# Products of ones on TensorE in four of its idle times, in a transformer block and mixture of experts on one core

## The reference

```python
def rmsnorm(x, g):
    y = xf * lax.rsqrt(jnp.mean(xf * xf, axis=-1, keepdims=True) + EPS)
    return (y * g.astype(jnp.float32)).astype(x.dtype)

def first_block(...):
    x = x + even_mixer(rmsnorm(x, e_norm[j]), ...)          # the first norm
    x = x + memory_cross_attention(rmsnorm(x, c_norm[i]), ...)
    ...
def second_block(...):
    x = x + merged @ w_out[l]
    h2 = rms_norm(x, ffn_norm_g[l])
    x = x + hierarchical_moe(h2, ...)                       # router, 32 experts, top 2
    return rms_norm(x, final_norm_g)                        # the last norm
```

## Time and profile before

| | |
|---|---|
| median of 3 runs | 1638.87 us (1638.64, 1643.22, 1638.87) |
| the profiled execution's own time | 1638.95 us |
| its span, first to last instruction | 1637.1 us |
| mean granted TensorE clock | 0.989 |
| PE busy | 1595.3 us (97%) |
| DVE, ACT, POOL busy | 845.6, 583.0, 547.6 us |

### The profile page before, as it was taken

How to read it: one execution, slowest core, us unless ns; L and a number is a source line. 1 busy time by engine, 2 the same in 40 slices (tenths; PEclk the granted TensorE clock), 3 DMA queues, 4 the chain that set the end, 5 groups by cost and what they waited for, 6 DMA issues and landing times.

```text
span 1637.1 us, 20086 instructions
## 1 busy us (share of the span) xinstructions
PE 1595.3 (97%) x7426; PEld 1203.3 (73%) x7426; DVE 845.6 (52%) x1456; ACT 583.0 (36%) x963; POOL 547.6 (33%) x239
## 2 busy tenths in 40 slices
PE   7999999999999999999999999999999999999997
PEld 5888768887888888887877667888877885444543
DVE  5447577125655546344668686343242644343434
ACT  4127454334332225324533342343243333112213
POOL 4441226731444444751334123455424410000000
PEclk9999999999999999999999999999999999999998
DMA  5331223521332323441222113334312349999991
GB/s 187 95 99 39 77 77 119 165 90 59 97 96 90 103 91 98 150 127 50 76 81 72 39 45 97 110 115 130 94 61 90 127 191 365 410 422 423 421 418 68
DMA packets 52787, 235.94 MB, mean 144 GB/s; under 512 B 6240, under 2 KB 7136, under 8 KB 48096
## 3 DMA queue, kind: packets, MB, share of 16 engines
q1 hardware_dynamic: 48960, 222.60, 38.8%
q0 software_dynamic: 2016, 7.34, 1.1%
q10 hardware_dynamic: 1728, 4.87, 0.9%
HBM read 230.59 MB, written 4.19 MB: 143 GB/s over the span
## 4 chain that ended last, share of the span: by engine, by line
PE 90%; DVE 6%; issue 2%; ACT 2%; DMA 0%; SPq 0%; DVEq 0%; ACTq 0%
PE G L1803 69%; PE O L1803 7%; PE S L1803 6%; PE TR L1803 4%; PE TR L1913 2%; DVE sumsq L993 1%; PE G L2370 1%; DVE sq L1053 1%; DMA w_ring<-in_stream_dram 0%; ACT hi_ring L569 0%; DVE U L1024 0%; DVE sumsq L1123 0%; DVE arena L1423 0%; DVE U L1780 0%; DVE arena L1202 0%
## 5 line engine op out<-in xcount | busy, mean ns | idle before, releaser
L534 POOL TENSOR_TENSOR lo_ring<-w_ring,hi_ring 128x1024 fp32r<-128x1024 f32 x219 | 533.9, 2439 | 788.9 <-ACT hi_ring L569 788.6
L569 ACT ACTIVATE hi_ring<-w_ring 128x1024 fp32r<-128x1024 f32 x219 | 231.3, 1059 | 588.7 <-PE G L1803 584.5
L1803 PE MATMUL G<-xa_hi,hi_ring 128*128 128x512 f32 x928 | 378.4, 408 | 9.7 <-DVE xa_lo L1115 9.6
L1803 PE MATMUL G<-xa_lo,hi_ring 128*128 128x512 f32 x928 | 364.6, 393 | 0.0
L1803 PE MATMUL G<-xa_hi,lo_ring 128*128 128x512 f32 x928 | 364.1, 392 | 0.0
L1803 PEld LDWEIGHTS G<-xa_hi,hi_ring 128*128 128x128 f32 x928 | 175.1, 189 | 50.1 <-issue 12.2
L1803 PEld LDWEIGHTS G<-xa_lo,hi_ring 128*128 128x128 f32 x928 | 175.1, 189 | 39.1 <-issue 2.6
L1803 PEld LDWEIGHTS G<-xa_hi,lo_ring 128*128 128x128 f32 x928 | 174.8, 188 | 39.4
L1803 PE MATMUL G<-yb_hi,hi_ring 128*128 128x512 f32 x388 | 154.4, 398 | 3.1 <-ACT arena L667 2.2
L1803 PE MATMUL G<-yb_hi,lo_ring 128*128 128x512 f32 x388 | 151.7, 391 | 0.0
L1803 PE MATMUL G<-yb_lo,hi_ring 128*128 128x512 f32 x388 | 151.3, 390 | 0.0
(11 more groups left out here) (350 smaller groups left out, 2503.8 us busy)
## 6 DMA issues: line engine op xcount, KB each, us to landing
w_ring<-in_stream_dram SPq DMA_DIRECT2D x219, 512.0 KB, 3.5
arena<-in_w_gu_dram SPq DMA_DIRECT2D x16, 2048.0 KB, 11.7
ex_rings<-in_w_dn_dram SPq DMA_DIRECT2D x40, 512.0 KB, 15.6
ex_low<-in_w_gu_dram SPq DMA_DIRECT2D x8, 2048.0 KB, 18.1
ex_rings<-in_w_gu_dram SPq DMA_DIRECT2D x8, 2048.0 KB, 15.7
arena<-in_w_dn_dram SPq DMA_DIRECT2D x16, 512.0 KB, 14.0
sq<-in_w_dn_dram SPq DMA_DIRECT2D x8, 512.0 KB, 17.6
X<-in_x_in_dram SPq DMA_DIRECT2D x8, 256.0 KB, 5.8
```

The source lines that it names most:

```text
L534: nc.gpsimd.tensor_tensor(lo_ring[:, s, :], w_ring[:, s, :], hi_ring[:, s, :], ALU.subtract).then_inc(low, 1)
L569: nc.scalar.activation(hi_ring[:, m % RING, :], w_ring[:, m % RING, :], ACT.Copy).then_inc(high, 1)
L1803: return nc.tensor.matmul(*args, **kw)
```

## The change

A helper issues products of a matrix of ones with itself, in plain float32, into a PSUM bank that nothing reads before it is written anew. It is called in four places (and with `final` once more in a branch that this input does not take): eight products of 512 columns ahead of everything else on PE, three of 256 ahead of the wait for the assignment, three of 256 between the rank products and the gather, and three of 256 between the last column sums and the last broadcast. Nothing waits for them, and they wait for nothing of their own.

```diff
+            def idle_products(bank, n, width):
+
+                for _ in range(n):
+                    mm(bank[:, 0:width * P].rearrange("p (a b) -> p a b", a=width), ones[:, :],
+                       ones[:, 0:P].unsqueeze(1).broadcast_to([P, width, P]), start=True, stop=True)
+
+            idle_products(S[:, 1, :], 8, 4)
+
             def three(out_ap, n, cols, hi, lo, first, last, weights_move=False):
...
             router(KT - 1)
             for f in range(4, KT):
                 rows(f)
+            idle_products(S[:, 1, :], 3, 2)
             pe.wait_ge(m_ready, 1)
             pe.wait_ge(rk_tab, 2)
...
                 ins.then_inc(col_full, 1)
+                idle_products(S[:, 1, :], 3, 2)
                 pe.wait_ge(diag, BC["f2"] + 1 + again)
                 mm(TR[:, :], ones[:, :], RB[:, :], start=True, stop=True).then_inc(bc_full, 1)
 
+            idle_products(O, 3, 2)
             gather_first()
             slots_first()
```

## The result

| | before | after |
|---|---|---|
| median | 1640.31 us (1637.46 to 1644.75, 22 runs) | 1644.24 us (1639.20 to 1646.91, 22 runs) |
| ratio | | 1.0017, 95% interval 1.0009 to 1.0025 |
| span of the profiled execution | 1637.1 us | 1642.5 us |

A forecast was written before the change was run, and what follows sets the result against it. PE, busy 97% of the span, was taken as the bound. Terms 0 - 0.75 + 0 and 0 = -0.75 on 1638.95 gave 1638.2, set to 1638.1 us as the median was 0.08 lower; range 1635.6 to 1641.0.

The forecast's parts named there:

- term 3: Fill between ranks and gather: clock holds, gather gains 1.8 us, slot table limits it; -0.75 us reaches the first expert products.
- Term 1: Eight products at the start: tile 1 ends about 1 us earlier, column sums still wait for the sum of squares; 0.
- Rival B: Clock falls at the first column sums as PE's wait there grows; +1.3 us, total 1639.4; chance 0.22.
- Terms 2 and 3: Fill ahead of the ranks hides in the assignment wait, 0; fill ahead of the gather keeps the clock up, -0.75 us.
- Term 4: Three products ahead of the last broadcast: fill at half clock ends 1.1 us late; taken as 0, between +1.1 and -1.0.
- C: Fills themselves run at half clock: gather ends +1.0 us, last fill +1.1, total 1641.0; chance 0.10.
- D: Falls at 216, 274 and 666 us, 1.7 us each, move: one or two vanish, 1636.4 or 1634.7, or one added; chance 0.15.
- E: No effect: clock falls at 1349.1 all the same, or experts' loads absorb the shift; 1638.9; chance 0.08.
- The Trainium skill's rule on transposes: Full clock "doesn't engage for transpose-mode": both rank fills would run at half clock, 1.0 us slower; given a small chance.

The follow-up runs named there:

- e15: Before plus twenty products of ones of 128 columns at the start, nothing elsewhere; executed once, 1643.59 us.
- e18: Before plus twenty products of ones of 128 columns behind the expert loop, ahead of the last broadcast; executed once, 1646.20 us.
- e8: Before plus fills at the start, ahead of the first column sums, three later norms' sums and one projection, and the two around the ranks; 1640.44 us, 0.9988.
- e14: The change plus two products of 256 columns between the gather and the slot products; 1642.49 us, 1.0001 of before.
- e17: The change unaltered, measured again against before; 1643.58 us, 1.0012.
- e1: Before plus only the change's eight products at the start; 1641.72 us, 1.0001.
- e3: Before plus only the change's three products ahead of the last broadcast; 1641.77 us, 1.0000.
- e11: Before plus the change's two fills around the ranks and two products of 256 columns ahead of the slot products; 1641.12 us, 0.9998.
- e10: e8 plus two products of 256 columns ahead of the slot products, without the last fill; 1639.39 us, 0.9985 of before.
- e9: The change plus two products of 512 columns ahead of the first column sums and two of 256 ahead of the slot products; 1640.06 us, 0.9989 of before.
- e16: Before plus twelve wide products in seven places, none at the start or ahead of the last broadcast; 1641.47 us, 1.0001.
- e4: Before plus the eight products at the start and two of 512 columns ahead of the first column sums; 1640.71 us, 0.9991.
- e5: Before plus only the change's start fill and last fill; 1642.33 us, 1.0005.
- e6: Before plus only fills ahead of three later norms' column sums and one projection; 1641.05 us, 0.9992.

## Why the prediction was wrong

The step that failed is the end of term 3: "**-0.75** reaches the first expert products" and "There PE is the bound to the end". The gain did reach the first expert products (-1.09 in the profile), and the loop behind them gave it back: rows that come 0.8 to 1.1 us late and, in some executions, a fall at its start. With it failed the level that all was added to, 1638.87, and of the loss itself 0.8 to 1.6 us stay open. By the ratio the change cost 2.8 us where the sum had -0.75.

**All profiles together** give what the two alone could not. Mean times, with the number of profiles (left out: e15's start, 32.80, with its own fill, and e18's end, where its fill stands):

| stretch | kernels | us |
|---|---|---|
| to the first broadcast's end | change's start fill, sums' wait not covered (5) | 34.62 |
| | neither (6, before among them; before 32.19) | 34.56 |
| | sums' wait covered (8) | 32.58 |
| `ffn` sums to first expert product | no fills at the ranks (9) | 23.04 |
| | fills there (11) | 22.23 |
| expert loop | rows on time (10) | 257.1 |
| | rows late, no fall (7) | 257.8 to 258.4 |
| | rows late and a fall at its start (3: e8, e14, e17) | 259.7 to 260.5 |
| last sums to the end | last fill (7) | 16.45 |
| | none (12) | 16.25 |

**Term 1, the start: 0.** Right, and so was its working: the sums start when they did and the second unit's low part is waited for. The mean to the first broadcast is the same with and without it (34.62 and 34.56), and e1 gives 1.0001.

**Rival B.** In the profiled execution it happened, where it was said. Its price was too low: the fall lasted 6.8 us and not 3.4, and cost 3.25 us instead of 1.3. In all profiles together a fall of 3.4 us here costs 1.6 and one of 6.8 costs 3.2: from the start of the sums to the end of the broadcast 7.5, 9.1 and 10.7 us. Its condition, "It decides as soon as tile 1 ends 1 us earlier", was not what sets the kernels apart. Of the twelve profiles without a cover here, the ten in which PE waited 1.62 to 2.35 us all had a fall within 2.4 us of the sums' start; before, with 1.49, had none, nor e15, where a fall at 18.6 us had slowed tile 1 and left a wait of 0.72. The eight covered ones waited 0.9 us or less and had none either. So the wait is the place, as the rival said. But half of the executions without the start fill (e3, e11, e18) already have the 2.3 us, and the others but one fell at 1.6 and 1.9. "At 24.66 nearly the same wait passed without a fall" took one execution for the rule. The sums near 273 us, which the rival had beside it, were the better guide: the same 1.39 us of wait was followed by a fall in 17 of 20 profiles. (e10, among the covered, has a fall at 17.8, ahead of the place.)

**The baseline.** The forecast stood on 1638.87, the median of three runs, and on a profile of 1638.95. In the comparison itself before's median was 1640.31, and the mean of 151 later runs is 1641.6: 1.4 to 2.7 of the 6.1 us between forecast and median. In those 151 runs the time follows the granted clock: 28 runs at 0.987 took 1643.5 us in the mean, 42 at 0.989 1641.3, 7 at 0.991 1638.3. So the spread goes with the falls, about 1.3 us for 0.001 of clock, and a sum made on one profiled execution carries an error as large as the range that I gave. Between kernels this does not hold. The change's 34 runs have a higher mean clock than before's 151 (0.9904 and 0.9886) and are slower all the same: at 0.990 it took 1644.4 us (10 runs) and before 1639.6 (28). Part of that is clock that PE had no use for: behind its last sums before's profile is at half clock for the last 14.7 us, the change's for 10.0. So the loss can't be read off the mean clock; what a fall costs depends on what PE does in it.

**Terms 2 and 3, ranks and gather: -0.75.** The clock held through both halves of the gather and the table set the start of the slot products, as worked out; the profile gave -1.09. (It held there in ten of the eleven profiles with these fills; e10 fell at 1349.0 and its first half took 5.73 us.) The clause that failed is "There PE is the bound to the end", for two reasons. The table's wait was named as the limit of the gain and not as a new idle time in which the clock could fall: in 3 of the 11 profiles with these fills it falls at the expert loop's start, which then takes 1.6 to 2.5 us more than with the late rows alone (259.7, 260.0 and 260.5 against about 258.0). And for the loop I looked only at the weights, with 2.1 us to spare even after the shift, not at the rows' fetch, which had 0.5.

**The late rows** stood in no term. The change adds 14 products ahead of the loop, and in both profiles of it PE waited for the rows, 0.8 and 1.1 us. The prediction asked where each product's time would be hidden, and not where its code would be loaded.

**Term 4, the last broadcast: 0.** Right within 0.2 us, and e3 gives 1.0000. The clock did not fall before the fill in the change but in it, at 1629.1, and the broadcast, 0.6 us behind its diagonal, took 1.91 us. In e9 it rose again while the broadcast ran: that took 1.42 us, behind a longer fill. In both the broadcast ends 6.8 us behind the start of the last sums; in before it was 7.0, in e10, without this fill, 6.4.

**The other rivals.** C fell: the fill ahead of the gather took 1.54 us, which is full clock, and at the start the clock rose 4.2 us into the program, so that fill took 8.76 us of the 9.4 predicted. D's falls at 216, 274 and 666 stayed in this execution and one was added, the sign that was put "inside the range". E's fall at 1349 came, but ahead of the gather, and cost it nothing.

**The Trainium skill's rule on transposes** ("TensorE: Matmul & The Clock Gate", Part 4): before showed the clock rise in them; in the change it fell in them (1349.1) and rose again in the fill at 1352.5. Over all profiles the traces disagree with that rule of the Trainium skill: the clock rose while the sixteen transposes ran in before, e3, e14 and e17, and in e10 they ran at full clock from first to last (1343.54 to 1345.48) and it stayed up until 1349.0.

**Adding up** by these means: 0 at the start, -0.8 at the ranks, +0.9 for the rows, about +0.9 for falls at the loop's start (2.5 and 2.0 us in two of the five profiles with the table's wait open), +0.2 at the end: +1.2 us, where the two measurements give 2.8 (1.5 to 4.1) and 2.0 (-0.2 to 3.9). The means rest on few profiles; the rest, 0.8 to 1.6 us, is open. It may lie between the first broadcast and the `ffn` sums, which took 1307.1 to 1311.6 us in the 20 profiles with none to four falls in it; the falls do not explain all of that either (before and e1, three each, took 1308.15 and 1311.27). The eight profiles with the change's start fill and no fill in that stretch took 1310.6 us in the mean, the five without any fill ahead of it 1309.2 (1307.3 to 1311.3): a difference of the right size that the spread does not let stand as shown.

The fastest kernel run is e10 at 0.9985, ahead of both, by a gain of 0.15% that e16, meant to keep it with fewer products, did not repeat.

## What to carry to other kernels

A fill that lets PE finish sooner can hand the idle time on to its next wait: before it goes in, ask what PE will wait for next, because a fall of the clock there can cost more than the one avoided. Find in a trace where each fill lands and whether the clock falls there at all; two of the fills here stood at sums that had no fall. Where a fill left 0.9 us or less of a wait ahead of column sums or a projection, no profile had a fall (19 of 19); at the slot table it was less sure (1 fall in 6). Instructions that compute nothing still have to be loaded, and where a transfer has tenths of a microsecond to spare, a dozen or so added products can bring a load of instructions into it. And where runs of the same kernel spread by 7 to 10 us while the granted clock moves with them, read several profiles of the same place before you price a fall.

## What was not expected of the hardware

- The clock's falls are not a property of the kernel alone: with the same PE program ahead of it, the stretch to the first broadcast took 32.19 us once and 33.6 to 36.3 us in five other profiles.
- A fall lasted 3.4 us in most places, 6.8 in others, and 13.7 at the gather of five kernels without the ranks' fills (e4, e5, e6, e15, e18). The same wait of 2.34 us ahead of the first sums was followed by 6.8 us in the change and by 3.4 in e1.
- One 16 KB packet of instructions went with a fetch that landed about 1 us later, in ten profiles of ten, and was absent from it in the ten where the rows were on time.
- Waits of 1.39 us ahead of a norm's column sums were followed by a fall of the clock in 32 of 40 places, waits cut to 0.9 us or less in none of 19.
- In plain float32 a product of 512 columns took 0.86 us at full clock at the first broadcast, and eight of them 8.76 us across the rise of the clock at 4.2 us.
